# Modulation vector of a two-block layer: its column sums kept apart by partition groups and summed at two seams

## The chip, the cores and the metric

The kernel runs on one core of a Trainium2 chip. The metric is the device time of one execution in microseconds (us). A core has TensorE (PE, with its weight loads shown apart as PEld), VectorE (DVE), ScalarE (ACT), GpSimd (POOL) and SyncE (SP), whose queue issues nearly all transfers here.

## The reference, cut to what matters

The layer has two blocks. The second one is modulated by six vectors of D = 2048 columns, all from one product of the row `silu(c)` (1 x 2048) with `w_ada` (2048 x 12288):

```python
def second_block(x, c, w_in, w_out, ...):
    c_act = jax.nn.silu(c)
    for l in range(DEPTH):
        mod = (c_act @ w_ada[l] + b_ada[l])[:, None, :]
        sh1, sc1, g1, sh2, sc2, g2 = jnp.split(mod, 6, axis=-1)
        h = rms_norm(x, norm_mix[l]) * (1.0 + sc1) + sh1
        x = x + g1 * hybrid_mixer(h, ...)
        h = rms_norm(x, norm_ffn[l]) * (1.0 + sc2) + sh2
        x = x + g2 * conv_glu_ffn(h, ...)
```

The first block (a mixer, then a gated FFN) comes ahead of it and does not use `mod`. All is float32; the large products are made from high and low parts of their operands, three products for one.

## The kernel before, in words

The stages follow one another on one core: first mixer (to about 420 us), gated FFN `Glu` (to 908 us), its down projection `Down` (to 1148 us), second mixer (to 1612 us), convolution FFN (to 2101 us), its `Down` and the end. Each stage streams its weights through four raw buffers; ACT makes the high part of a half buffer (L289), DVE the low part (L297), three units ahead of the PE. Each engine's order is written out in the code by unit numbers; SP's order is written out too.

The product with `w_ada` runs beside them. Its 12288 columns are 12 groups ("leads") of 1024. For a group, class `Ada` loads 16 row blocks of 128 x 1024 in eight transfers of 1 MB (`load`, L498), and DVE multiplies each block by 128 values of `silu(c)`, one for a partition, and adds it to a 128 x 1024 accumulator (`product`, L516 and, for the first block, L518). The accumulator then has to be summed over its 128 partitions. Group 0 is gathered in the first mixer, groups 1 to 5 in `Glu`, 6 to 8 in `Down`, 9 in the second mixer, 10 and 11 in the convolution FFN. The sum is made in three ways:

- groups 0 to 5 (`turned`, `reduced`): right after the group, between two units of `Glu`, the PE transposes the accumulator in eight 128 x 128 pieces (L460) and DVE reduces them (L467) to eight columns of `modcols`;
- groups 6 and 7 (`Down.ada_sums`, L1953): at the seam from `Down` to the second mixer (here: seam 1), eight products with a column of ones each, and one addition of the bias by DVE at L1963. Group 8's accumulator is stored to memory there;
- groups 8 and 9 at the seam from the second mixer to the convolution FFN (seam 2): L3616 with ones, L460 by transposes; groups 10 and 11 by 128 x 512 products later (L3646).

Around seam 1 the order is: the PE's last products of `Down` (L1875), the sums, four early transposes (L2152), the rest of the sums, four transposes (L2141) that wait for rows scaled by ACT (L2117) and DVE (L2130), then the first products of the second mixer (L2216). DVE makes the mean there (L3172 to L3179), the factors 1 + scale (`modulation`, L3547) and a reciprocal (L3183) that waits for ACT's root (L2954). Seam 2 is built alike (L3745 to L3754, L2152, L2141, L608), with three idle transposes (L449, `keep_busy`) ahead of L2141. In the first mixer small vectors are loaded as rows (`packs`, tile `pack`), transposed by the PE one pack for a unit (L945) and copied by DVE to `col` (L1332).

## Time and profile before

| | |
|---|---|
| median of 3 runs | 2351.67 us (2350.42 to 2352.06) |
| profiled execution | 2352.51 us, span 2350.7 us |
| mean granted TensorE clock | 0.997 |
| PE busy | 2337.8 us, 99% |
| PEld busy | 2151.6 us, 92% |
| DVE busy | 1616.4 us, 69% |
| ACT busy | 1153.2 us, 49% |
| DMA | 543.62 MB, mean 231 GB/s |

The span runs from the first to the last instruction; 1.8 us of the execution's time lie outside it. The PE is busy nearly throughout. Records of matmuls overlap, so the time that one costs in a stream is read from the starts or from the chain of waits, not from its own duration.

### The profile page before, as it was taken

How to read it: one execution, taken by the hardware profiler on the slowest of the kernel's cores; microseconds unless marked ns; L12 is line 12 of the kernel's file. 1: busy time of each engine (PE TensorE's matmuls, PEld its weight loads, DVE VectorE, ACT ScalarE, POOL GpSimd, SP SyncE). 2: the span in 40 equal slices, each digit the busy share in tenths (PEclk: the TensorE clock that was granted, in tenths of full speed). 3: DMA queues.
4: the chain of work that ended last, by engine and by line, in shares of the span. 5: the costliest groups of instructions: out<-in, count | busy, mean ns of one | idle time of the engine just before them, and what ended most of it. 6: DMA issues, size and time to landing. Idle time of an engine off the chain costs nothing.

```text
span 2350.7 us, 43754 instructions
## 1 busy us (share of the span) xinstructions
PE 2337.8 (99%) x17937; PEld 2151.6 (92%) x17937; DVE 1616.4 (69%) x1931; ACT 1153.2 (49%) x1510; POOL 5.1 (0%) x7
## 2 busy tenths in 40 slices
PE   9999999999999999999999999999999999999998
PEld 8889778999999999888999899888999999998887
DVE  5668568777777766877778455667878666665556
ACT  5565454534344344444764444546544445454444
POOL 0000000000000000000000000000000000000000
PEclk9999999999999999999999999999999999999999
DMA  8556567888888877898577545555778656665563
GB/s 308 167 179 197 159 234 271 278 282 297 282 282 295 282 242 263 316 324 315 175 279 269 163 130 153 196 200 187 283 255 295 208 179 206 196 206 197 192 192 117
DMA packets 233049, 543.62 MB, mean 231 GB/s; under 512 B 15610, under 2 KB 22596, under 8 KB 232260
## 3 DMA queue, kind: packets, MB, share of 16 engines
q1 hardware_dynamic: 232756, 540.97, 68.3%
q8 instruction: 110, 1.80, 0.3%
q10 hardware_dynamic: 144, 0.52, 0.1%
q14 instruction: 39, 0.32, 0.0%
HBM read 535.11 MB, written 6.32 MB: 230 GB/s over the span
## 4 chain that ended last, share of the span: by engine, by line
PE 98%; DVE 0%; ACT 0%; issue 0%; DMA 0%; SPq 0%; DVEq 0%; ACTq 0%
PE ps L330 37%; PE ps L1858 18%; PE ps L608 18%; PE ps L2216 16%; PE ps L1875 2%; PE ps L2509 0%; PE ps L1041 0%; PE ps L1053 0%; PE ps L1071 0%; PE ps L1083 0%; PE ps L2141 0%; PE ps L460 0%; PE ps L2744 0%; PE ps L1134 0%; PE ps L2921 0%
## 5 line engine op out<-in xcount | busy, mean ns | idle before, releaser
L297 DVE TENSOR_TENSOR weights_lo<-raw_weights,weights_hi 128x1024 fp32r<-128x1024 f32 x786 | 957.6, 1224 | 659.8 <-ACT weights_hi L289 658.0
L289 ACT ACTIVATE weights_hi<-raw_weights 128x1024 fp32r<-128x1024 f32 x782 | 827.2, 1062 | 1086.8 <-PE ps L330 446.4
L516 DVE SCALAR_TENSOR_TENSOR ada_acc<-ada_w,col,ada_acc 128x1024 f32<-128x1024 f32 x180 | 230.2, 1279 | 0.1
L330 PE MATMUL ps<-conv_x_hi,weights_hi 128*128 128x256 f32 x1280 | 198.0, 277 | 0.0
L330 PE MATMUL ps<-glu_x_hi,weights_hi 128*128 128x256 f32 x1280 | 197.7, 276 | 0.0
L330 PE MATMUL ps<-glu_x_hi,weights_lo 128*128 128x256 f32 x1280 | 197.2, 276 | 0.0
L330 PE MATMUL ps<-glu_x_lo,weights_hi 128*128 128x256 f32 x1280 | 197.2, 276 | 0.0
L330 PE MATMUL ps<-conv_x_lo,weights_hi 128*128 128x256 f32 x1280 | 197.2, 276 | 0.0
L330 PE MATMUL ps<-conv_x_hi,weights_lo 128*128 128x256 f32 x1280 | 197.2, 276 | 0.0
L330 PEld LDWEIGHTS ps<-conv_x_hi,weights_hi 128*128 128x128 f32 x1280 | 169.1, 188 | 1.0 <-issue 1.0
L330 PEld LDWEIGHTS ps<-glu_x_hi,weights_hi 128*128 128x128 f32 x1280 | 169.0, 188 | 0.0
L330 PEld LDWEIGHTS ps<-glu_x_lo,weights_hi 128*128 128x128 f32 x1280 | 168.9, 188 | 0.0
L330 PEld LDWEIGHTS ps<-glu_x_hi,weights_lo 128*128 128x128 f32 x1280 | 168.9, 188 | 0.0
L330 PEld LDWEIGHTS ps<-conv_x_hi,weights_lo 128*128 128x128 f32 x1280 | 168.9, 188 | 0.0
L330 PEld LDWEIGHTS ps<-conv_x_lo,weights_hi 128*128 128x128 f32 x1280 | 168.9, 188 | 0.0
L2216 PE MATMUL ps<-m_x_hi,weights_hi 128*128 128x256 f32 (+1 forms) x576 | 94.9, 288 | 0.1
L3800 DVE SCALAR_TENSOR_TENSOR conv_y<-ps,conv_taps,conv_y 128x255 f32<-128x255 f32 (+1 forms) x176 | 72.7, 476 | 29.8 <-ACT conv_y L3732 28.8
L2216 PE MATMUL ps<-m_x_lo,weights_hi 128*128 128x256 f32 (+1 forms) x576 | 89.8, 279 | 0.0
L2216 PE MATMUL ps<-m_x_hi,weights_lo 128*128 128x256 f32 (+1 forms) x576 | 89.2, 277 | 0.5 <-issue 0.5
L1858 PE MATMUL ps<-weights_hi,down_hi 128*128 128x512 f32 x288 | 89.0, 390 | 0.5 <-DVE stat L3804 0.2
L1858 PE MATMUL ps<-weights_hi,down_lo 128*128 128x512 f32 x288 | 88.7, 389 | 0.0
L1858 PE MATMUL ps<-weights_lo,down_hi 128*128 128x512 f32 x288 | 88.7, 389 | 0.0
(560 smaller groups left out, 3635.3 us busy)
## 6 DMA issues: line engine op xcount, KB each, us to landing
raw_weights<-in_w_in_dram SPq DMA_DIRECT2D x202, 512.0 KB, 5.0
ada_w<-in_w_ada_dram SPq DMA_DIRECT2D x96, 1024.0 KB, 6.1
raw_weights<-in_w_ffn_up_dram SPq DMA_DIRECT2D x176, 512.0 KB, 4.6
raw_weights<-in_w_gate_dram SPq DMA_DIRECT2D x88, 512.0 KB, 4.6
raw_weights<-in_w_up_dram SPq DMA_DIRECT2D x88, 512.0 KB, 4.6
raw_weights<-in_w_down_dram SPq DMA_DIRECT2D x88, 512.0 KB, 5.7
raw_weights<-in_w_ffn_down_dram SPq DMA_DIRECT2D x88, 512.0 KB, 4.3
raw_weights<-in_w_out_dram SPq DMA_DIRECT2D x64, 512.0 KB, 5.1
```

The lines of the kernel that those rows point to most:

```text
L289: kit.nc.scalar.activation(kit.slots(n, i)[0], raw, ACT.Copy).then_inc(kit.w_hi, 1)
L297: kit.nc.vector.tensor_tensor(lo, raw, hi.bitcast(F32), ALU.subtract).then_inc(kit.w_lo, 1)
L330: ins = nc.tensor.matmul(out, lhsT=lhsT, rhs=rhs, start=start and m == 0, stop=(k == KT - 1 and m == 2), skip_group_check=True)
L516: step = nc.vector.scalar_tensor_tensor(acc, w, c, acc, ALU.mult, ALU.add)
L608: ins = nc.tensor.matmul(out, lhsT=lhsT, rhs=rhs, start=start and m == 0, stop=ends and m == 2, skip_group_check=True)
L1858: ins = nc.tensor.matmul(kit.ps[:, 4 * t + 2 * half + q, :], lhsT=lhsT, rhs=rhs, start=(k == 0 and m == 0), stop=ends and m == 2, skip_gro ...
L1875: ins = nc.tensor.matmul(kit.ps[:, 4 * t + 2 * half + q, :], lhsT=lhsT, rhs=w[:, q * UN:(q + 1) * UN], start=False, stop=k == w_tiles - 1 ...
L2216: ins = nc.tensor.matmul(out, lhsT=lhsT, rhs=rhs, start=start and m == 0, stop=ends and m == 2, skip_group_check=True)
L3800: nc.vector.scalar_tensor_tensor(y[:, j, q, b:S], self.tile(j, q)[:, 0:S - b], taps[:, j, tap, q:q + 1], y[:, j, q, b:S], ALU.mult, ALU.ad ...
```

## The change

Groups 0 to 7 now share one accumulator. Partition 16g + r belongs to group g: each transfer brings 16 rows of `w_ada` with the first 8192 columns, cut by group into 8 x 16 partitions, and the multiplier is a column in which 16 values of `silu(c)` are repeated eight times (`c_oct`, 128 such columns). After 128 steps one set of eight products with an indicator (`oct`, 128 x 8) gives all 64 columns. Groups 8 and 9 share another accumulator by halves (`c_half`, `half`, 128 x 2) in the same manner; its first half stays in the accumulator that is continued in the second mixer. Groups 10 and 11 are as before. The sums between the units of `Glu` and the additions of the bias behind them go. The 16 columns of a group are copied to a fixed tile in `Glu` (`c_turn`), since its loop counts groups. Each 1 MB transfer becomes two of 512 KB with a semaphore of their own. In the first mixer one more pack (`c_oct`, 128 x 128) is transposed one unit after the last; it waits until DVE has repeated its rows in the tile `pack` and copied the pack ahead of it.

```diff
     def load(self, sp, lead, j, m):
-        sp.dma_start(self.w[:, m % 2, :, :], w[2 * m * P:2 * (m + 1) * P, ds(2 * UN * lead + 2 * UN * j, 2 * UN)]
-                     .rearrange("(k p) n -> p k n", p=P)).then_inc(kit.ada_w[m % 2], 16)
+        for s in (2 * m, 2 * m + 1):
+            sp.dma_start(self.w[:, m % 2, s % 2, :], self.source(lead, j, s)).then_inc(kit.ada_w[s % 4], 16)
...
+    def source(self, lead, j, s):
+        w = self.kit.ins["w_ada_2"][0]
+        if lead < 8:
+            rows = w[ds(OCT * (16 * lead + s) + 16 * OCT * j, OCT), 0:16 * UN]
+        elif lead < 10:
+            rows = w[HALF * (16 * (lead - 8) + s):HALF * (16 * (lead - 8) + s + 1), 16 * UN:20 * UN]
...
+        return rows.rearrange("r (g n) -> g r n", n=2 * UN)
...
+    def sums(self, pe, bank, mask, acc):
+        kit, (a, b) = self.kit, self.kit.at[mask]
+        n = b - a
         for q in range(8):
+            step = kit.nc.tensor.matmul(kit.ps[:, bank, n * q:n * (q + 1)], lhsT=acc[:, q * P:(q + 1) * P],
+                                        rhs=kit.c(mask), start=True, stop=True)
...
-            mid = (lambda: self.ada.turned(pe, self.lead, j)) if summed else None
-                if summed and s == begun:
-                    self.ada.reduced(dve, self.lead, j)
                 if half is not None and s % 2 == begun:
-                    self.ada.product(dve, self.lead, j, 8 * half + s // 2)
+                    q = 8 * half + s // 2
+                    if q == 0:
+                        a = COLS["c_oct"] + 16 * self.lead
+                        dve.wait_ge(kit.ada_acc, 16 * self.lead + 16 * j)
+                        nc.vector.tensor_copy(self.c_turn[:, :], kit.col[:, ds(a + 16 * j, 16)]).then_inc(self.s_c, 1)
+                        dve.wait_ge(self.s_c, 1 + j)
+                    self.ada.product(dve, self.lead, j, q, c=self.c_turn[:, q:q + 1])
...
     def sync(self, sp):            # Down
-        sp.wait_ge(kit.ada_sum, self.lead)
-        sp.dma_start(self.final_w[:, :], self.final_src).then_inc(kit.loaded, 16)
+                if k == 12:
+                    sp.wait_ge(kit.ada_acc, 16 * self.lead + 1)
+                    self.load_final(sp)
...
     def pack_out(self, dve, n):
+        if n == len(self.packs) - 2:
+            dve.wait_ge(self.s_packs, 16 * sum(len(p[0]) for p in self.packs[1:]))
+            self.kit.nc.vector.tensor_copy(self.pack[:, 0, :].rearrange("p (g r) -> p g r", r=OCT),
+                                           self.c_rows[:, :].unsqueeze(1).broadcast_to([P, P // OCT, OCT])
+                                           ).then_inc(self.s_cwide, 1)
...
     def vector(self, dve):         # second mixer
+        self.down.ada_summed(dve)
         modulation(kit, 0)
...
     def scale_sums(self, pe):
-        for q in range(8):
-            step = kit.nc.tensor.matmul(kit.ps[:, 1, q:q + 1], lhsT=mixer.accs[:, 0, q * P:(q + 1) * P],
-                                        rhs=kit.c("ones")[:, 0:1], start=True, stop=True)
-        step.then_inc(kit.ada_sum, 1)
-        pe.wait_ge(mixer.s_xlast, ST)
-        turn_sums(kit, mixer.accs[:, 1, :], 2).then_inc(kit.ada_sum, 1)
+        pe.wait_ge(self.mixer.s_accs, 16)
+        pe.wait_ge(self.kit.pair_free[0], self.uses[0] + 1)
+        self.ada.sums(pe, 1, "half", self.mixer.acc_back)
```

The PE's order in `Glu`, between two units (names: `ps` the accumulation banks, `cst` the constants with the identity, `glu_x_hi/lo` the stage's operand). Before:

```order
L330 MATMUL ps<-glu_x_lo,weights_hi 128x256 x4
L330 MATMUL ps<-glu_x_hi,weights_lo 128x256 x4
L460 MATMUL ps<-cst,ada_acc 128x128 [waits ada_acc]
L460 MATMUL ps<-cst,ada_acc 128x128 x7
L330 MATMUL ps<-glu_x_hi,weights_hi 128x256 [waits weights_lo]
```

and at the same place now:

```order
L335 MATMUL ps<-glu_x_lo,weights_hi 128x256 x4
L335 MATMUL ps<-glu_x_hi,weights_lo 128x256 x4
L335 MATMUL ps<-glu_x_hi,weights_hi 128x256 [waits weights_lo]
L335 MATMUL ps<-glu_x_hi,weights_hi 128x256 x3
L335 MATMUL ps<-glu_x_lo,weights_hi 128x256 x4
```

The eight transposes have gone and nothing stands in their place. The PE's order at seam 1 (`m_scaled` are the rows to be transposed). Before:

```order
L1875 MATMUL ps<-down_last_hi,glu_x_lo 128x512
L1953 MATMUL ps<-cst,ada_acc_98 128x1 [waits ada_acc,square_sums,first_sems_cleared]
L1953 MATMUL ps<-cst,ada_acc_98 128x1 x7
L1953 MATMUL ps<-cst,ada_acc_99 128x1 x2
L2152 MATMUL ps<-cst,m_scaled_126 128x128 [waits rows_scaled0,square_sums]
L2152 MATMUL ps<-cst,m_scaled_126 128x128 [waits rows_scaled0] x3
L1953 MATMUL ps<-cst,ada_acc_99 128x1 x6
L2141 MATMUL ps<-cst,m_scaled_126 128x128 [waits rows_scaled1,rows_scaled0]
L2141 MATMUL ps<-cst,m_scaled_126 128x128
```

and now:

```order
L1873 MATMUL ps<-down_last_hi,glu_x_lo 128x512
L513 MATMUL ps<-cst,ada_acc_oct 128x8 [waits ada_acc,square_sums,first_sems_cleared]
L513 MATMUL ps<-cst,ada_acc_oct 128x8 x7
L2139 MATMUL ps<-cst,m_scaled_127 128x128 [waits rows_scaled0,square_sums]
L2139 MATMUL ps<-cst,m_scaled_127 128x128 [waits rows_scaled0] x3
L2128 MATMUL ps<-cst,m_scaled_127 128x128 [waits rows_scaled1,rows_scaled0]
L2128 MATMUL ps<-cst,m_scaled_127 128x128
```

Half of the sums have gone, among them all that stood between the early transposes and the waiting ones. DVE's order at the same seam, before and now (one piece each; `modT` holds the factors, `stat` the statistics):

```order
L3179 SCALAR_TENSOR_TENSOR stat<-stat 128x1 [waits square_sums,dve_order]
L3547 SCALAR_TENSOR_TENSOR modT<-modcols,col 128x16
L3183 RECIPROCAL stat<-stat 128x2 [waits m1_x_in0,dve_order]
L2130 TENSOR_SCALAR m_scaled_126<-x_weighted,stat 128x256 [waits token_scales] x2
L2130 TENSOR_SCALAR m_scaled_127<-x_weighted,stat 128x512 [waits token_scales]
```

```order
L3160 SCALAR_TENSOR_TENSOR stat<-stat 128x1 [waits square_sums,dve_order]
L523 TENSOR_TENSOR modcols<-ps,col 128x8x8 [waits ada_sum]
L3526 SCALAR_TENSOR_TENSOR modT<-modcols,col 128x16 [waits ada_out]
L3165 RECIPROCAL stat<-stat 128x2 [waits c_rows_repeated,dve_order]
L2117 TENSOR_SCALAR m_scaled_127<-x_weighted,stat 128x256 [waits token_scales] x2
```

The addition that brings the sums out of `ps` stands ahead of the factors, and the factors wait for it.

## Rows read from the trace of the kernel before

**Rows 1.** The page, part 1: busy time (share of the span) and instructions.
```profile
PE 2337.8 (99%) x17937; PEld 2151.6 (92%) x17937; DVE 1616.4 (69%) x1931; ACT 1153.2 (49%) x1510; POOL 5.1 (0%) x7
```
**Rows 2.** The page, part 4: the chain that ended last, shares by engine.
```profile
PE 98%; DVE 0%; ACT 0%; issue 0%; DMA 0%; SPq 0%; DVEq 0%; ACTq 0%
```
**Rows 3.** The chain in `Glu`, in order of time: start us, us, what.
```profile
514.28 0.87 PE ps L460 x8
515.16 87.12 PE ps L330 x768
602.27 0.87 PE ps L460 x8
...
867.12 40.87 PE ps L330 x360
```
**Rows 4.** The accumulator's instructions: ns min/median/max, first and last start us.
```profile
L516 DVE SCALAR_TENSOR_TENSOR ada_acc<-ada_w,col,ada_acc x180: 1273/1279/1287, 342.2 to 1827.2; 128x1024 f32<-128x1024 f32 x180
...
L460 PE MATMUL ps<-cst,ada_acc x48: 272/273/273, 427.8 to 866.8; 128*128 128x128 f32 x48
...
L518 DVE TENSOR_SCALAR ada_acc<-ada_w,col x12: 744/746/749, 337.7 to 1744.2; 128x1024 f32<-128x1024 f32 x12
```
**Rows 5.** `Glu` by windows: us, PE, PEld, DVE, ACT, POOL, PEclk, DMA share, GB/s.
```profile
510.00:900.00 390.00, 390.00 (x3441) 390.00 (x3441) 284.27 (x238) 158.66 (x152) 0.00 (x0) 1.00 0.80 276
```
**Rows 6.** The page, part 6: the transfers of `w_ada`.
```profile
ada_w<-in_w_ada_dram SPq DMA_DIRECT2D x96, 1024.0 KB, 6.1
```
**Rows 7.** The chain at seam 1.
```profile
1147.75 2.12 PE ps L1953 x20
1149.87 0.50 PE ps L2152 x4
1150.37 2.08 PE ps L1953 x12
1152.45 0.95 PE ps L2141 x4
```
**Rows 8.** DVE at seam 1, timeline.
```profile
1150.21 0.17 DVE L3547 SCALAR_TENSOR_TENSOR modT<-modcols,col 128x16 f32<-128x16 f32 x1
1150.63 0.17 DVE L3183 RECIPROCAL stat<-stat 128x2 f32<-128x2 f32 x1 [0.25 <-ACT stat L2954]
1150.83 1.01 DVE L2130 TENSOR_SCALAR m_scaled<-x_weighted,stat 128x256 f32<-128x256 f32 x3
```
**Rows 9.** Seam 1 by windows, columns as in Rows 5.
```profile
1147.30:1149.60 2.30, 2.30 (x21) 2.22 (x21) 2.03 (x6) 1.98 (x5) 0.00 (x0) 1.00 0.01 4
...
1150.60:1153.40 2.80, 2.80 (x13) 2.41 (x13) 1.18 (x4) 1.14 (x3) 0.00 (x0) 0.50 0.96 228
1153.40:1157.20 3.80, 3.74 (x18) 3.74 (x18) 3.70 (x8) 3.20 (x6) 0.00 (x0) 0.50 0.84 319
```
**Rows 10.** The chain at seam 2.
```profile
1612.57 1.68 PE ps L3616 x16
1614.25 0.93 PE ps L460 x8
1615.18 0.33 PE ps L449 x3
...
1615.63 0.32 PE ps L2141
```
**Rows 11.** Seam 2 by windows, columns as in Rows 5.
```profile
1612.30:1615.60 3.30, 3.21 (x30) 2.97 (x28) 2.50 (x11) 1.54 (x4) 0.00 (x0) 1.00 0.72 225
1615.60:1619.00 3.40, 2.88 (x20) 2.44 (x21) 2.87 (x8) 3.03 (x7) 0.00 (x0) 1.00 0.64 249
```
**Rows 12.** Seam 2, DVE, then the PE's next weight load, timeline.
```profile
1614.36 0.17 DVE L3627 TENSOR_TENSOR modcols<-ps,col 128x8 f32<-128x8 f32 x1 [0.50 <-PE ps L3616]
1614.44 0.15 DVE L3749 SCALAR_TENSOR_TENSOR stat<-stat 128x1 f32<-128x1 f32 x1
...
1615.60 0.47 PEld L2141 LDWEIGHTS ps<-cst,conv_scaled 128*128 128x128 f32 x4 [0.33 <-ACT conv_scaled L2117]
```
**Rows 13.** First mixer: the transposition of a pack in the chain.
```profile
57.95 0.08 PE ps L945
```
**Rows 14.** First mixer, DVE timeline: the copy of the last pack.
```profile
60.28 0.25 DVE L1332 COPY col<-ps 128x96 f32<-128x96 f32 x1
```
**Rows 15.** First mixer, PE timeline: the unit after next begins.
```profile
60.65 0.61 PE L608 MATMUL ps<-weights_hi,m_x_hi 128*128 128x512 f32 x2
```

More of the change, by code:

```diff
@@ L503, in product, with scalar @@
+    def scalar(self, lead, s):
+        name, first = ("c_oct", 0) if lead < 8 else ("c_half", 8) if lead < 10 else ("c_2", lead)
+        return self.kit.cols(name, 16 * (lead - first) + s)
+    def product(self, dve, lead, j, s, acc=None, prior=None, c=None):
         nc, kit = self.kit.nc, self.kit
         m, k = s // 2, s % 2
-        if s == 0 and self.stored:
-            dve.wait_ge(kit.ada_sum, lead - 1)
-            dve.wait_ge(self.stored, 16)
-        elif s == 0 and lead and acc is None:
-            dve.wait_ge(kit.ada_sum, lead + j)
@@ L827, in sync @@
         for n in range(1, len(self.packs)):
-            for at, to, width, src in self.packs[n][0]:
-                sp.dma_start(self.pack[at:to, n, 0:width], src).then_inc(self.s_packs, 16)
+            tile = self.c_rows if n == len(self.packs) - 1 else self.pack[:, n, :]
+            for at, to, lo, hi, src in self.packs[n][0]:
+                sp.dma_start(tile[at:to, lo:hi], src).then_inc(self.s_packs, 16)
         bias = self.mem["bias_dram"].ap()
@@ L944, in turn_pack @@
         _, w, _ = self.packs[n]
-        kit.nc.tensor.transpose(kit.ps[:, 6, 0:w], self.pack[0:w, n, :], kit.c("ident")[0:w, 0:w]
-                                ).then_inc(self.s_packT, 1)
+        last = n == len(self.packs) - 1
+        if last:
+            pe.wait_ge(self.s_cwide, 1)
+        rows = self.pack[0:w, 0 if last else n, :]
+        kit.nc.tensor.transpose(kit.ps[:, 6, 0:w], rows, kit.c("ident")[0:w, 0:w]).then_inc(self.s_packT, 1)
     def spread_scale(self, at):
@@ L3263, in vector_side @@
         if n in self.ADA:
-            self.ada.product(dve, self.lead, 0, self.ADA.index(n))
+            s = self.ADA.index(n)
+            self.ada.product(dve, self.lead, 0, s, prior=None if s else self.down.accs[1])
     def added_out(self, dve, p):
@@ L3825, in program @@
         junk = t("y_squares", 80, [P, ST, D])
-        accs = [t(f"ada_acc_{6 + n}", a, [P, 2 * UN])[:, :] for n, a in enumerate((56, 60, 106))]
+        accs = [t(f"ada_acc_{n}", a, [P, 2 * UN])[:, :] for n, a in (("oct", 56), ("half", 60))]
         def wide_head(w):
```

222 lines of the change are left out of this document (83 added, 139 removed).

## The prediction

> **What bounds the kernel now.** I read the page's shares first: the PE is busy for 99% of the span, DVE for 69% [rows 1]. A busy PE is not proof, so the chain of waits comes second: 98% of it is PE work [rows 2]. Only what shortens the PE's own list, or one of the few places where it waits, can move the time. The chain in `Glu` shows what a sum between two units costs: 87.12 us of stage products, then 0.87 us for eight transposes, then products again, with no idle time between them [rows 3]. The last places to read are the two seams, where the order of small steps decides [rows 7 to 12].
>
> **The change part by part.**
>
> *Transposes between units of `Glu`.* There are 48 in the accumulator's list, so six sets of eight, one for each of the groups 0 to 5 [rows 4]. Each set takes 0.87 us of the chain [rows 3]. All of it is on the path: 6 x 0.87 = 5.2 us. Nothing takes their place in the order. What is late next would be the weights' low parts from DVE, but DVE is busy for 284 of 390 us in this stage, and the PE waited for nothing in it (390.00 us busy) [rows 5]. So I count the whole 5.2 us as gained, with bounds of 4.8 (a little given back at the joints) and 5.3.
>
> *DVE's share.* Six reductions and one at seam 2 go. Eight first steps become additions: 1279 instead of 744 to 746 ns, + 0.53 us each [rows 4]. A copy of 16 columns and a wait for it come for each of five groups. In `Glu` this is about even for each group and lies under the PE's stream, with 106 us of DVE's time free there [rows 5]. In `Down` and the second mixer three first steps, 1.6 us, are spread over 700 us. Cost 0; if the cover were gone, at most the 1.6 us and the copies.
>
> *Transfers.* 80 of the 96 transfers of 1 MB [rows 6] read other addresses, all 96 become two. A piece for one partition remains 4 KB, and the bytes are the same. The DMA engines are busy for 0.80 of `Glu` [rows 5]. Cost 0, with the bound as a rival below.
>
> *Seam 1, the PE.* Before, 20 records of thin products, four early transposes, 12 more records, then the transposes that wait for scaled rows [rows 7]. Each product shows as two records. Twenty records took 2.12 us of the chain, 106 ns each; 12 records took 2.08 us, 173 ns each, because the granted clock fell from 1.00 to 0.50 (2.4 to 1.2 GHz) at about 1150.6, after three microseconds in which the PE had made hardly anything but one-column products [rows 7, 9]. Now 16 records remain, all ahead of the early transposes. With 8 columns instead of one I take the same 106 ns, since the weight load is the same; if the columns counted, seven more for each record would still be a small part of the 128 of a transpose, at 109 ns (0.87/8) [rows 3]. So the sums end 0.4 us earlier, and the early transposes are followed directly by the waiting ones. DVE begins to scale the second rows at 1150.83 in three steps of together 1.01 us [rows 8], the first third done at about 1151.17. The waiting transposes began in the chain at 1152.45 because the thin products still stood ahead of them [rows 7]. They can now start at about 1151.3, plus what DVE adds.
>
> *Seam 1, DVE.* The addition of 64 columns and its wait now stand ahead of the factors and the reciprocal. DVE was idle for 0.25 us there, until ACT's root came [rows 8]. The addition is like the 0.17 us steps around it, plus some 0.1 us for 64 strided elements and about 0.1 us for the wait: 0.3 to 0.4 us, of which the idle time hides 0.25. I take + 0.1, at most + 0.4. Queued behind it are the reciprocal and the scaled rows, for which the PE waits.
>
> *Seam 1, sum.* In hand: between the first piece of scaled rows (1151.2) and the end of the thin products (1152.45) lie 1.25 us, less 0.2 for the handover, less 0.1 for DVE: about 0.95 at most. From there the PE runs at half the clock until about 1157.3 [rows 9]. If that end stays where it is, an earlier start is worth half of itself, 0.45; if it moves along, 0.95. Without any fall of the clock before, there would be about 0.1 in it. I take - 0.5, bounds 0 and - 1.0.
>
> *Seam 2.* The eight transposes (0.93 us) went before three idle ones and 0.33 us of waiting for scaled rows [rows 10, 12]. Without them the PE waits longer at the same place: gain 0. The 16 thin records remain. DVE's addition (1614.36) now has to finish before the next step of the mean (1614.44, 0.08 us later) [rows 12]: that step starts after the addition's 0.17 us and hands on, so the chain mean, root, reciprocal, scaled rows, PE is late by 0.1 us. Cost + 0.1, bounds 0 and + 0.2. The reduction and the second set of factors that stood later on DVE there go, under PE work.
>
> *First mixer.* One more pack is transposed: 0.1 us, as the 0.08 of the one before [rows 13]. It stands one unit later, and the next unit started at 60.65 [rows 15]. DVE starts the copy of the pack before at 60.28 (0.25 us) [rows 14]. Ahead of it now stands the copy that repeats the rows, of the same kind and size, so both are done at about 60.85, and the PE waits 0.25 us. Together + 0.35, bounds + 0.1 and + 0.6. Three more small transfers on SP's queue and one activation of 160 columns lie in units whose weights are made three units (8 us) ahead: 0.
>
> *Entry of `Down`.* A wait for the additions and the addition go. The chain has no more than 0.1 us in it: 0.
>
> Sum: - 5.2 - 0.5 + 0.1 + 0.35 = - 5.25 us; I take - 5.1, since handovers rather cost than give. Against the profiled execution (2352.5 us) that is 2347.4; it was 0.8 us above the median of the runs, so against this (2351.7) it is 2346.6.
>
> **The clock at seam 2, the rival that the sum hides.** In seam 2 the clock stayed at 1.00 through 3.3 us of thin products, transposes and a short wait, and through the next 3.4 us [rows 11]. In seam 1 it fell after thin products that were broken only by four transposes (0.50 us) [rows 7, 9]. The change takes out of seam 2 just the eight transposes that stood between thin products and waiting, and leaves 1.7 us of thin products, 0.33 us of idle transposes and about 1.3 us of waiting. So it may fall there now. The price from seam 1: 3.8 us of dense work at half the clock before it rose [rows 9], half of it lost, 1.9 us. The time would be 2346.6 + 1.9 = 2348.5.
>
> The Trainium skill ("TensorE: Matmul & The Clock Gate", Part 4: PE-mode transpose) says that transposes do not count as busy for the clock as products do. By that, seam 2 was as quiet before as it is now, and the change would not make a fall there likelier. This trace has one row for each side: four transposes did not keep the clock at seam 1, eight more stood in seam 2 where it stayed. The rule alone would leave the sum as it is and lower the chance of this rival.
>
> **Other rivals.**
> - *More at seam 1* (chance 0.08): with the thin products halved, the clock does not fall there. The 3.8 us of dense work at half the clock [rows 9] would give back 1.9 us, and the first transposes (0.95 for four, against 0.5 for four early ones [rows 7]) another 0.4: about 2344.3. For it: less thin work. Against: what replaces it is waiting.
> - *The stream was held by something else* (0.05): if the sets of transposes covered time that DVE needed, the PE would wait at the same joints and most of the 5.2 us would come back: about 2351. Against: no wait of the PE in `Glu`, DVE 73% busy [rows 5].
> - *Slower* (0.03): the transfers in eight column pieces of 16 rows run slower. From one set of transposes to the next (88 us) some 24 MB come at 276 GB/s [rows 3, 5], and 8 of them are a group of `w_ada`: a third, 0.27 of the 0.80 share. Once they take over 1.75 times as long, the share passes 1 and the PE waits; at twice as long it is 1.07, and the 470 us of `Glu` grow by 7%, 33 us: 2380. Against: the pieces stay at 4 KB and their rows lie closer together.
>
> **How the numbers follow.** Forecast as summed: 0.6; the clock falls at seam 2: 0.24; the others 0.08, 0.05, 0.03. The likeliest case gives 2346.6. The bounds of its terms add to - 6.2 at one end (- 5.3 - 1.0 + 0 + 0.1) and - 4.0 at the other (- 4.8 + 0 + 0.2 + 0.6), and the runs shown differ by 1.6 us among themselves. With the clock rivals on either side the range is 2344.7 to 2349.4. A change of 0.2%, 4.7 us, is about what a measurement of this kernel can tell from none, and the forecast lies just beyond it, below 2347.0. Of the forecast's 0.6 I put 0.45 beyond it, with the 0.08 and a few hundredths of the rest: faster 0.57, within 0.2% 0.40, slower 0.03.
>
> **What would show it.** Right: in `Glu` the chain shows products without a break and the PE busy to the full; `Down` begins 5.2 us earlier, less what the first mixer added, so at about 903.3; seam 1, from the last dense product to the first of the second mixer, is shorter by about 0.9 us; the PE's wait ahead of the first waiting transposes at seam 2 grows from 0.33 to about 1.3 us. Wrong: a clock of 0.50 in seam 2 beside a gain under 4 us; a wait of the PE for DVE's low parts in `Glu`; transfers of `w_ada` whose two halves take clearly more than the 6.1 us of the whole [rows 6]; a wait of over 0.5 us for the repeated rows in the first mixer.

## The result, and the profile after

The changed kernel took 2873.7 us in the median (2857.1 to 2891.9), the kernel before 2351.8 in the same comparison: a ratio of 1.222, 95% interval 1.214 to 1.231. Forecast were 2346.6 us. It is not slightly slower, it is 522 us slower, and the forecast had given "slower" a chance of 0.03. The profiled execution took 2857.1 us, its span is 2855.3.

The page of the changed kernel, part 1 (answers to [rows 1]), the shares of part 4 by engine ([rows 2]), and two lines of part 6 ([rows 6] and a kind of stage weights):
```profile
PE 2481.5 (87%) x17866; PEld 2259.3 (79%) x17866; DVE 1603.4 (56%) x1927; ACT 1149.0 (40%) x1511; POOL 5.1 (0%) x7
...
PE 52%; DMA 35%; DVE 6%; SPq 4%; issue 2%; ACT 1%; DVEq 0%; ACTq 0%
...
ada_w<-in_w_ada_dram SPq DMA_DIRECT2D x192, 512.0 KB
...
raw_weights<-in_w_gate_dram SPq DMA_DIRECT2D x88, 512.0 KB, 18.0
```
The chain was 98% PE work; now transfers make 35% of it. The stage weights, which the change does not touch, need 18.0 us from issue to landing for the gate, 18.9 and 18.4 for `w_up` and `w_down`; in the kernel before the page had 4.6, 4.6 and 5.7 for them. For `ada_w` the page gives no landing time.

The chain of the changed kernel inside `Glu` (answers to [rows 3]), and what waited for `ada_w` in the whole kernel (us in total, times):
```profile
611.02 20.58 DMA ada_w<-in_w_ada_dram
...
635.18 1.28 DVE ada_acc L505
636.46 2.28 DVE weights_lo L302 x2
...
639.53 21.32 DMA ada_w<-in_w_ada_dram
```
```profile
  DVE ada_acc L505: 382.0, 56
  DVE ada_acc_half L505: 145.8, 15
```
The chain stays on one transfer for 20 to 21 us. DVE stands at its accumulating instruction, in program order the low parts of the weights are behind it, and the PE is behind those. The accumulating instruction itself is what it was: 1283 ns against 1279 [rows 4].

Windows of the changed kernel, columns as in [rows 5]: `Glu`, and the time of groups 8 and 9. Then the head of the DMA view of the second window in 40 slices (tenths of the mean share of 16 engines; GB/s):
```profile
510.00:900.00 390.00, 312.89 (x2445) 308.64 (x2446) 203.99 (x177) 112.26 (x107) 0.00 (x0) 0.89 0.79 207
1310.00:1490.00 180.00, 91.70 (x266) 68.83 (x265) 45.53 (x46) 24.82 (x32) 0.00 (x0) 0.71 0.32 106
```
```profile
DMA  3111541111951113511118711117211158111159
GB/s 100 53 53 52 164 129 54 53 53 71 283 183 53 52 56 134 162 53 53 52 52 249 237 53 52 52 53 218 83 53 53 53 181 284 76 53 56 53 180 270
```
This is the telling pair of rows. In `Glu` the share is as before (0.79 against 0.80 [rows 5]) while the bytes fall from 276 to 207 GB/s. Later the DMA engines look idle, a tenth busy, and the rate stands still at 52 or 53 GB/s for many slices. Two of sixteen engines are 0.125 of the share, and 53 GB/s over two are 26.5 GB/s each; e1 below reaches 406 GB/s in one slice of 5 us, 25.4 for each of sixteen. So in those slices two engines work at their full rate and fourteen stand. The source of groups 8 and 9 has the group as its outermost dimension, of size 2; that of groups 0 to 7 has it at 8.

The two rows of windows say different things. Fewer engines at their full rate lower the share and the rate together: 106 GB/s at 0.32 are 331 GB/s for a full share, near the 345 (276 / 0.80) of `Glu` before. In the changed `Glu` it is 207 / 0.79, 262. There the engines were also slower for each byte; how much is worked out under e3 and e4.

The queue that issues the transfers was held up as well. The transfers of `ada_w` in the second window (issue time in ns, least, median, most), and a piece of SP's timeline there:
```profile
L487 SPq DMA_DIRECT2D ada_w<-in_w_ada_dram x13: 787/9849/12712, 1308.7 to 1461.7; - x13
...
1344.12 14.44 SPq L258 DMA_DIRECT2D raw_weights<-in_w_down_dram  x4
1358.60 11.94 SPq L487 DMA_DIRECT2D ada_w<-in_w_ada_dram  x2
```
To issue one took 9.8 us in the median, which is what 512 KB need at 53 GB/s (9.9 us); in e1 below it is 346 ns. Stage weights are issued by the same queue, so they came late in two ways: issued late and, once issued, landed late.

The Trainium skill says it outright ("DMA: Bandwidth & Descriptors", "Why a DMA increments its semaphore by 16 and not by 1", How many engines): the number of engines is the largest up to 16 that divides the slowest dimension of both access patterns, and they are the lowest-numbered ones. By that, 8 and 2 engines; for 2 the 53 GB/s at a tenth of the share agree, for 8 no row shows the number of engines by itself. The prediction had not weighed this rule.

### The profile page after: what moved, and what is told of

Read it like the earlier page. It is cut to its first block, busy times and chain, and to the rows that moved or that the text cites. A ratio compares the mean times of both kernels' runs of the same rounds, so it can differ in the third digit from the quotient of the medians.

```text
span 2855.3 us, 43835 instructions
## 1 busy us (share of the span) xinstructions
PE 2481.5 (87%) x17866; PEld 2259.3 (79%) x17866; DVE 1603.4 (56%) x1927; ACT 1149.0 (40%) x1511; POOL 5.1 (0%) x7
## 4 chain that ended last, share of the span: by engine, by line
PE 52%; DMA 35%; DVE 6%; SPq 4%; issue 2%; ACT 1%; DVEq 0%; ACTq 0%
DMA ada_w<-in_w_ada_dram 28%; PE ps L335 17%; PE ps L579 11%; PE ps L2203 10%; PE ps L1856 8%; DVE weights_lo L302 3%; DMA raw_weights<-in_w_in_dram 3%; SPq L258 3%; DMA raw_weights<-in_w_out_dram 2%; PE ps L1873 1%; DVE ada_acc L505 1%; SPq L487 1%; DMA raw_weights<-in_w_gate_dram 1%; DMA raw_weights<-in_w_down_dram 1%; DVE ada_acc_oct L505 0%
## 5 line engine op out<-in xcount | busy, mean ns | idle before, releaser
L335 PE MATMUL ps<-glu_x_hi,weights_hi 128*128 128x256 f32 x1280 | 221.8, 299 | 111.9 <-DVE weights_lo L302 111.9
L335 PEld LDWEIGHTS ps<-glu_x_hi,weights_hi 128*128 128x128 f32 x1280 | 189.2, 208 | 118.3 <-DVE weights_lo L302 115.1
L505 DVE SCALAR_TENSOR_TENSOR ada_acc<-ada_w,glu_c,ada_acc 128x1024 f32<-128x1024 f32 x80 | 102.6, 1282 | 287.8 <-DMA ada_w<-in_w_ada_dram 285.4
L335 PE MATMUL ps<-glu_x_lo,weights_hi 128*128 128x256 f32 x1280 | 214.1, 293 | 0.0
L335 PE MATMUL ps<-glu_x_hi,weights_lo 128*128 128x256 f32 x1280 | 212.2, 291 | 0.0
L335 PE MATMUL ps<-conv_x_hi,weights_hi 128*128 128x256 f32 x1280 | 198.0, 277 | 0.0
L335 PE MATMUL ps<-conv_x_lo,weights_hi 128*128 128x256 f32 x1280 | 197.2, 276 | 0.0
L335 PE MATMUL ps<-conv_x_hi,weights_lo 128*128 128x256 f32 x1280 | 197.2, 276 | 0.0
L335 PEld LDWEIGHTS ps<-glu_x_lo,weights_hi 128*128 128x128 f32 x1280 | 186.5, 205 | 0.0
L335 PEld LDWEIGHTS ps<-glu_x_hi,weights_lo 128*128 128x128 f32 x1280 | 184.4, 203 | 0.0
L335 PEld LDWEIGHTS ps<-conv_x_hi,weights_hi 128*128 128x128 f32 x1280 | 169.1, 188 | 1.0 <-issue 1.0
L335 PEld LDWEIGHTS ps<-conv_x_lo,weights_hi 128*128 128x128 f32 x1280 | 168.9, 188 | 0.0
L335 PEld LDWEIGHTS ps<-conv_x_hi,weights_lo 128*128 128x128 f32 x1280 | 168.9, 188 | 0.0
L505 DVE SCALAR_TENSOR_TENSOR ada_acc<-ada_w,col,ada_acc 128x1024 f32<-128x1024 f32 x60 | 76.8, 1280 | 109.1 <-DMA ada_w<-in_w_ada_dram 95.4
L1856 PE MATMUL ps<-weights_hi,glu_x_hi 128*128 128x512 f32 x192 | 71.9, 461 | 75.5 <-DVE weights_lo L302 75.5
L2203 PEld LDWEIGHTS ps<-m_x_hi,weights_hi 128*128 128x128 f32 (+1 forms) x576 | 88.0, 211 | 53.3 <-DVE weights_lo L302 50.9
L1856 PEld LDWEIGHTS ps<-weights_hi,down_hi 128*128 128x128 f32 x288 | 57.2, 204 | 71.3 <-issue 58.8
L1856 PEld LDWEIGHTS ps<-weights_hi,glu_x_hi 128*128 128x128 f32 x192 | 41.7, 225 | 89.3 <-issue 81.0
## 6 DMA issues: line engine op xcount, KB each, us to landing
raw_weights<-in_w_up_dram SPq DMA_DIRECT2D x88, 512.0 KB, 18.9
raw_weights<-in_w_down_dram SPq DMA_DIRECT2D x88, 512.0 KB, 18.4
```

What stands on the lines that cost most here:

```text
L335: ins = nc.tensor.matmul(out, lhsT=lhsT, rhs=rhs, start=start and m == 0, stop=(k == KT - 1 and m == 2), skip_group_check=True)
L505: step = nc.vector.scalar_tensor_tensor(acc, w, c, acc if prior is None else prior, ALU.mult, ALU.add)
L1856: ins = nc.tensor.matmul(kit.ps[:, 4 * t + 2 * half + q, :], lhsT=lhsT, rhs=rhs, start=(k == 0 and m == 0), stop=ends and m == 2, skip_gro ...
L2203: ins = nc.tensor.matmul(out, lhsT=lhsT, rhs=rhs, start=start and m == 0, stop=ends and m == 2, skip_group_check=True)
```

## The experiments

All were compared with the kernel before on the same chip (2351.6 to 2354.8 us in the median). Theory after the result: the outermost dimension sets the number of engines. Rivals: the rows' addresses, the doubled number of transfers, or something on PE or DVE.

**e1_plain_rows.** Everything of the change stays except the source of the transfers: groups 0 to 9 read plain blocks of 128 rows, so the sums are not those of the reference.
```
-        if lead < 8:
-            rows = w[ds(OCT * (16 * lead + s) + 16 * OCT * j, OCT), 0:16 * UN]
-        elif lead < 10:
-            rows = w[HALF * (16 * (lead - 8) + s):HALF * (16 * (lead - 8) + s + 1), 16 * UN:20 * UN]
+        if lead < 10:
+            rows = w[P * s:P * (s + 1), ds(2 * UN * lead + 2 * UN * j, 2 * UN)]
```


> The changed kernel with one thing different: every transfer of w_ada for groups 0 to 9 reads 128 whole rows of one group's 1024 columns, as groups 10 and 11 do (same 512 KB, same tile, same count and order of transfers; the accumulated values are therefore not those of the reference). Theory A (a transfer whose address pattern has 8 or 2 as its slowest dimension runs on 8 or 2 of the 16 DMA engines, and all of the lost time comes from that): 2346 to 2348 us, the forecast of the prediction, PE clock 0.997, no wait of DVE for ada_w. Theory B (twice the number of transfers, each half as large, with issues and semaphores of their own, is what costs): still far above 2352, near 2870. Theory C (the seams or the shared accumulator cost part of it): 2355 to 2450.

2347.4 us, ratio 0.9981 (0.9971 to 0.9991). All 526 us hang on how `w_ada` is read; twice as many transfers cost nothing that shows beside the forecast (2346.6), and the rest of the change is worth some 4.2 us. The transfers of `ada_w` land after 5.4 us by the page, and `Glu` is undisturbed:
```profile
510.00:900.00 390.00, 390.00 (x3444) 390.00 (x3443) 283.22 (x240) 161.47 (x153) 0.00 (x0) 1.00 0.81 278
```

**e2_rows_slowest.** The whole reference, with the row as outermost dimension: 16 rows x 8 pieces, so partition 8r+g instead of 16g+r; groups 8 and 9 as two transfers of 64 rows to 64 partitions each.
```
-        return rows.rearrange("r (g n) -> g r n", n=2 * UN)
+        return rows.rearrange("r (g n) -> r g n" if lead < 8 else "r (g n) -> g r n", n=2 * UN)
...
+                for g in range(2):
+                    sp.dma_start(self.w[HALF * g:HALF * (g + 1), m % 2, s % 2, :], src[g]).then_inc(kit.ada_w[s % 4], 16)
```


> The changed kernel with the same bytes of w_ada read from the same addresses into the same number of partitions, but with the rows as the slowest dimension. Groups 0 to 7: partition 8r + g instead of 16g + r (indicator and repeated multipliers follow), so the transfer's slowest dimension is 16 instead of 8. Groups 8 and 9: layout as it was, each 512 KB transfer made as two of 64 rows, so 64 instead of 2. It computes all of the reference. Theory A (number of engines by the slowest dimension): 2346 to 2350 us; half transfers issue 32 more times on SP, hidden. Theory D (the addresses: 16 or 64 rows of 48 KB pitch with 4 KB pieces side by side are slow to read): stays near 2870, at most a little better.

2440.3 us (2409.9 to 2454.7), ratio 1.033 (1.027 to 1.040). Neither theory had this: A had said 2346 to 2350, D near 2870. Sixteen as outermost dimension gives back 433 of the 526 us, but 93 remain. Its `Glu`, from a run with a span of 2452.9 us, the longest of its four:
```profile
510.00:900.00 390.00, 365.10 (x3100) 361.29 (x3101) 259.02 (x226) 145.90 (x140) 0.00 (x0) 0.98 0.98 263
```
The share is 0.98 for 263 GB/s, where e1 moved 278 with 0.81: a full set of engines, each slower. That is a second effect. The profile of e5 below, from the fastest of its runs, which has the same eight-group transfers and plain ones for groups 8 and 9, shows it too:
```profile
510.00:900.00 390.00, 368.84 (x3169) 365.14 (x3168) 260.39 (x227) 146.81 (x141) 0.00 (x0) 0.99 1.00 264
```

**e3_oct_only** and **e4_half_only.** The changed kernel with groups 8 and 9 plain, and with groups 0 to 7 plain.
```
e3:  -            rows = w[HALF * (16 * (lead - 8) + s):HALF * (16 * (lead - 8) + s + 1), 16 * UN:20 * UN]
     +            rows = w[P * s:P * (s + 1), ds(2 * UN * lead + 2 * UN * j, 2 * UN)]
e4:  -            rows = w[ds(OCT * (16 * lead + s) + 16 * OCT * j, OCT), 0:16 * UN]
     +            rows = w[P * s:P * (s + 1), ds(2 * UN * lead + 2 * UN * j, 2 * UN)]
```

> The changed kernel with groups 8 and 9 read as whole rows (values not those of the reference); groups 0 to 7 keep eight column pieces of 16 rows. It prices the 128 transfers with slowest dimension 8. Theory A: 8 of 16 engines carry 1 MB of w_ada and 1 MB of stage weights for each group of about 88 us, against 1.5 MB before, and bursts of a transfer take twice as long; the traced stage from 424 to about 1095 us in the changed kernel suggests about 2352 + 165 (FFN) + 25 (mixer) + 60 (down, two of three groups) = 2600 us. The stretch of groups 8 in the down projection becomes normal.

> The changed kernel with groups 0 to 7 read as whole rows (values not those of the reference); groups 8 and 9 keep two column pieces of 64 rows. It prices the 32 transfers with slowest dimension 2. Theory A: 512 KB over 2 engines at about 26.5 GB/s each is 9.9 us for a transfer, and the stage's own weights queue behind on these two engines; 32 transfers cost about 32 x 9.9 = 320 us less what is hidden, so about 2600 us; the sum of the two excesses (this one and that of the run with groups 0 to 7 alone) equals the whole 520 us within 10%. In that stretch the transfer rate stands at 53 GB/s.

2608.5 us (ratio 1.110) and 2606.0 (1.108). Above e1 these are 261 and 259 us, together 520 of the 526: two separate losses of one kind, the smaller volume on the fewer engines costing as much. In `Glu`, e4 is undisturbed (1.00, 0.81 and 278 as in e1) and e3 is not; a stretch of e4, 1200 to 1400 us, shows the 52 GB/s again in the DMA view:
```profile
510.00:900.00 390.00, 297.89 (x2297) 293.21 (x2297) 189.38 (x165) 107.02 (x103) 0.00 (x0) 0.89 0.79 194
```
```profile
GB/s 62 261 172 52 56 52 162 255 254 53 48 13 354 386 95 82 208 218 202 121 199 3 344 314 386 61 139 144 52 52 52 156 215 52 52 53 223 143 138 51
```
What the transfers cost the engines can be read from part 3 of the pages (packets, MB, share of 16 engines), e1, e3 and e4:
```profile
q1 hardware_dynamic: 234260, 539.96, 68.6%
...
q1 hardware_dynamic: 233236, 539.95, 68.3%
...
q1 hardware_dynamic: 233812, 539.96, 62.3%
```
The bytes are the same. Times the spans (2345.9, 2642.5 and 2602.7 us) these are 1609, 1805 and 1622 us of all sixteen engines. The 67 MB of groups 0 to 7 cost about 196 us at e1's rate in `Glu` (278 GB/s at 0.81), and e3 adds 196 to them: transfers with 8 outermost took about twice the engine time for each byte, beside being on half of the engines. The 17 MB of groups 8 and 9 cost 49 us and e4 adds 12: with 2 outermost the time for a byte grew by about a quarter. These are estimates from rounded shares.

**m1_sixteen_rows, m2_halves_and_turned, m3_engines.** To find the second effect, each kernel issues four kinds of transfer in turn, each from its own line, for groups 0 to 5, and plain ones for 6 to 9. The sums are not the reference's, and each of these kernels ran once; a kind has 24 transfers. The sources of m1's kinds 1 to 3, and m2's kind 1:
```
w[ds(16 * (16 * L + s) + 256 * j, 16), 0:16 * UN]   "r (g n) -> r g n"                    # 16 rows, adjacent
w.rearrange("(r q) c -> r q c", q=128)[:, 16 * L + s + 16 * j, 0:16 * UN]  "-> r g n"      # 16 rows, 128 apart
w[ds(...), :]  "r (g n) -> r g n" with n=3 * UN, [:, :, 0:2 * UN]                          # pieces 6 KB apart
w[128 * s:128 * (s + 1), ...]  "(m i) c -> i m c" with i=16                                # turned block
```


> Four ways of reading w_ada side by side in one kernel, in the pairs of transfers issued at the same instant (each 2 x 512 KB, 16 engines), for the groups before Down; every kind has its own line, and each kind comes twice in a group of 16. The values are not the reference's. Kinds: 0 plain blocks of 128 rows; 1 sixteen adjacent rows, eight adjacent pieces of 4 KB from each (as in e2_rows_slowest); 2 sixteen rows that lie 128 rows apart, eight adjacent pieces; 3 sixteen adjacent rows, eight pieces that lie 6 KB apart. In e1_plain_rows a transfer landed 5.4 us after its issue, in e2_rows_slowest 15.4. Theory N (what slows the engines is that all 16 read from rows that lie close together): kinds 1 and 3 land late, 9 us or more, kinds 0 and 2 at 5 to 6.5. Theory C (what slows them is that one engine reads 32 KB in a row of adjacent addresses): kinds 1 and 2 land late, kinds 0 and 3 early. Time of the kernel: between those of the two, 2350 to 2400 us.

> As m1_sixteen_rows, with other kinds: 0 plain blocks of 128 rows, of which an engine reads eight adjacent rows; 1 the same blocks turned, so that engine i reads rows i, 16+i, 32+i and so on, and the 16 engines stand on 16 adjacent rows at any time; 2 sixty-four adjacent rows, two pieces each; 3 sixty-four rows that lie 32 rows apart, two pieces each. Theory N: it is the place of the 16 engines at one time that counts, so kind 1 lands late like the sixteen rows (9 us or more) although it reads the plain blocks; kind 2 somewhat late (7 to 12), kind 3 at 5 to 6.5. Theory B (bytes of a transfer drawn from a small stretch of w_ada, whoever reads them): kind 1 like kind 0 at 5 to 6.5, kind 2 late. Time 2348 to 2390 us.

> As m1_sixteen_rows, with other kinds: 0 plain (slowest dimension 128); 1 as in the changed kernel, slowest dimension 8, sixteen adjacent rows; 2 slowest dimension 8, sixteen rows 128 rows apart; 3 slowest dimension 4, thirty-two adjacent rows and four pieces. Theory E (the slowest dimension sets the number of engines, each at its full rate of some 26 GB/s): a pair of 1 MB takes 1 MB / (8 x 26 GB/s) = 5 us on eight engines and 10 us on four, beside the stage weights that wait on the same engines; so kinds 1 and 2 land later than kind 0 by a factor of two, kind 3 by a factor of four. If nearness adds to it, kind 1 lands later than kind 2 by half again; if not, the same. Time 2450 to 2700 us.

Landing times by line (least, median, most us) of m1: kinds 0, 1, 2, 3:
```profile
DMA to landing us min/median/max: 3.8/5.7/9.6
...
DMA to landing us min/median/max: 5.0/6.9/16.1
...
DMA to landing us min/median/max: 5.6/7.5/13.2
...
DMA to landing us min/median/max: 4.4/5.4/10.1
```
The same of m2: plain, turned, 64 rows near, 64 rows spread:
```profile
DMA to landing us min/median/max: 4.0/5.8/9.9
...
DMA to landing us min/median/max: 5.0/7.3/16.5
...
DMA to landing us min/median/max: 4.5/5.8/9.8
...
DMA to landing us min/median/max: 4.0/5.7/7.8
```
Both theories of addresses fall. Rows 128 apart are as slow as adjacent ones (7.5, 6.9), which N forbids; adjacent rows with pieces 6 KB apart are as fast as plain (5.4). C fits m1, but the turned block of m2 has no adjacent pieces and is slow (7.3). B said that it would be like plain, and falls too. What the three slow kinds share is a source that begins with a dimension of exactly 16; the fast "6 KB apart" has one even stride over all 128 pieces, so its dimensions can fold into 128. That they do is read from its issue time on SP, 345 ns in the median as for plain (348), where the slow kinds take 556 to 569. The landing times were lower than I had written (9 us), I take it because only a part of the transfers is slow here. The kernels took 2346.5 and 2347.3 us, less than the 2350 and 2348 that I had put as their least. The windows of `Glu` of m1 and of m2 show what they occupy:
```profile
510.00:900.00 390.00, 390.00 (x3444) 390.00 (x3443) 283.32 (x239) 160.66 (x152) 0.00 (x0) 1.00 0.88 278
```
```profile
510.00:900.00 390.00, 390.00 (x3444) 390.00 (x3443) 283.50 (x239) 160.65 (x152) 0.00 (x0) 1.00 0.85 277
```
`w_ada` is 0.27 of the share, one kind of four 0.07. Two slow kinds add 0.07 and one adds 0.04: each takes 1.5 to 1.6 times as long. All of it at 1.6 would make 0.81 + 0.16 = 0.97. e2 shows 0.98 and e5 1.00, but at 263 and 264 GB/s instead of 278; for each byte that is a `w_ada` at 1.8 to 1.9 times. So where all of it is slow, it is slower still.

m3 took 2550.9 us. Its transfers on 8 and 4 engines have no landing row, but DVE's waits for each kind have:
```profile
  DVE ada_acc L514: 13.5, 6
...
  DVE ada_acc L514: 65.5, 18
...
  DVE ada_acc L514: 92.4, 12
...
  DVE ada_acc L514: 125.0, 22
```
Plain, outermost 8 with rows near, 8 with rows 128 apart, 4: the order is that of the number of engines. Between the two eights nothing is decided: the one with rows 128 apart is issued right before and right after the transfers on 4 engines, whose issue alone takes 3.7 us in the median, and its waits may hold part of theirs. Factors of two and four, as I had written them, cannot be read from it.

**m4_sixteen_chunks, e5_oct_sixteen_engines, e6_half_one_transfer, e7_split_plain.** The theory now is P: the writing side. By it the 16 engines write to 16 separate places when the first dimension is 128; with exactly 16, or with only 64 partitions, pairs of engines would write through one port. m4's kind 2 keeps the plain addresses but does not fold; e7 keeps the plain addresses and cuts a transfer of groups 8 and 9 at partition 64; e6 puts 64 rows x 2 pieces in one transfer.
```
m4, kind 1:  w[32 rows, 0:8 * UN]    "r (g n) -> r g n"                       # 32 x 4
m4, kind 2:  w[144 rows, ...]        "(i k) n -> i k n" with k=9, [:, 0:8, :] # 16 x 8
e6:          w[64 rows, 16 * UN:20 * UN]  "r (g n) -> r g n"                  # 64 x 2
e7:          w[P * s:P * (s + 1), ...]    "(g r) n -> g r n" with g=2, one transfer for each g
```


> As m1_sixteen_rows, again four kinds of transfer side by side on lines of their own, all on 16 engines. m1 and m2 showed: sixteen rows of eight adjacent pieces are slow whether the rows are adjacent or 128 apart (7.5 and 6.9 us in the median against 5.7), plain blocks turned so that the slowest dimension is 16 are slow too (7.3), while 16 adjacent rows of pieces 6 KB apart (which fold into one even dimension of 128) and 64 rows of two pieces are not (5.4, 5.8). Kinds here: 0 plain (dimension 128); 1 thirty-two adjacent rows, four adjacent pieces (dimensions 32 x 4); 2 sixteen chunks of eight adjacent rows of which every ninth is left out (16 x 8: the addresses nearly those of the plain block, but the dimensions do not fold); 3 as kind 3 of m1 with every second row (16 x 8, does not fold either). Theory P (a source whose slowest dimension is exactly 16 gives each engine eight neighbouring partitions in the kernel's memory to write, and the engines get in each other's way at writing; where the rows lie makes no difference): kinds 2 and 3 land late at about 7 us or more, kind 1 as kind 0. Theory A (the addresses read decide): kind 2 like kind 0, kind 3 like kind 3 of m1, both at 5.3 to 6. Time 2345 to 2352 us.

> e2_rows_slowest with groups 8 and 9 read as whole blocks of 128 rows, one transfer each (their values are then not the reference's): only the eight-group transfers keep the slowest dimension 16. The 93 us that e2_rows_slowest stands above e1_plain_rows split into the share of the eight groups and that of the two halves. Both theories: most of it belongs to the eight groups, since PE stood idle from 500 to 1150 us there. 2405 to 2435 us.

> e1_plain_rows with groups 8 and 9 read as 64 rows of two pieces, the row as slowest dimension (64), in one transfer of 128 partitions; groups 0 to 7 plain (values not the reference's). From kind 2 of m2 (5.8 us as the plain blocks): 2346 to 2349 us by theory P as well as by theory A. If it is over 2352, 64 x 2 has a cost that m2 did not show.

> e1_plain_rows with each transfer of groups 8 and 9 cut in two, of 64 partitions each, as in e2_rows_slowest, but of the whole blocks' rows: what is read is what e1 reads, and only the 64 partitions that each transfer writes are as in e2 (11.3 us from issue to landing there, 5.4 in e1). Values not the reference's. Theory P (the writing side): landing of these transfers 8 us or more although their addresses are plain; the kernel some microseconds over e1: 2350 to 2375. Theory A (addresses read): landing 4 to 6, kernel 2346 to 2349.

m4 (2347.3 us), kinds 0 to 3, then e7's transfers to 64 partitions:
```profile
DMA to landing us min/median/max: 4.6/5.6/9.9
...
DMA to landing us min/median/max: 3.9/5.4/12.8
...
DMA to landing us min/median/max: 5.5/7.5/11.0
...
DMA to landing us min/median/max: 5.5/7.2/11.4
```
```profile
DMA to landing us min/median/max: 3.9/10.1/19.1
```
Both 16 x 8 kinds are slow (7.5, 7.2), one of them at nearly plain addresses, the other being m1's fast kind 3 with its fold broken; 32 x 4 is not (5.4). The kinds stand in the same places of a group as in m1, where kind 1 was slow and kind 3 fast, so the place is not the cause. (The expectation of m4 gives m1's two values in the wrong order: adjacent rows took 6.9, rows 128 apart 7.5.) Theory A falls: the addresses that are read do not decide. Plain addresses written to 64 partitions at a time take 10.1 us, where e1's transfers of the same groups took 5.5. This is weaker than it looks, since e7 also has twice as many transfers of half the size there, and no run has those without the 64 partitions.

e7 as a whole: 2354.7 us (2345.9 to 2364.4), ratio 1.0013 (0.9999 to 1.0027), 7 us over e1. e6: 2347.1 us, ratio 0.9981, as e1: 64 rows x 2 costs nothing. e5: 2424.3 us (2411 to 2443), ratio 1.034 (1.029 to 1.039). So the eight groups alone cost 77 us over e1. How much of e2's 93 belongs to the halves cannot be read from the times, whose ratios are the same (1.033 and 1.034). The traces do show a part: DVE waits for the halves' transfers 33.1 us in e2 and 1.9 in e5.

That it is the ports rests on shapes and not on a row that names a port. The Trainium skill ("SBUF — State Buffer", "Door 1: The DMA port swizzle") puts partitions four by four on sixteen ports and p and p+32 on the same one; the Trainium skill ("DMA: Bandwidth & Descriptors", "The descriptor swizzle") gives each engine in a 128-partition transfer a port of its own. If engine i has the neighbouring partitions 8i to 8i+7 instead, engines i and i+4 begin on one port; with 64 partitions only eight ports are in use. Both would give up to a factor of two. The shares show 1.5 to 1.9, the landing times 1.2 to 1.3 for the four kinds and 1.8 for e7. The same reasoning covers the changed kernel. With partition 16g + r, and engine g taking group g, engines 0 and 2 write to partitions 0 to 15 and 32 to 47, which are the same ports, while the two engines of the halves (0 to 63, 64 to 127) share none. The 2.0 and 1.2 worked out above fit that. Which engine writes where, and why 32 x 4 and 64 x 2 escape, no row shows.

**e8_half_rows.** A version from this: 32 half rows x 4 pieces, so that groups 0 to 3 and 6 to 9 share the first accumulator and no outermost dimension is 16; groups 4 and 5 as 64 rows x 2. They are the gate of the second mixer, so their sums move there.
```
+            halves = w.rearrange("r (h c) -> (r h) c", h=2)
+            rows = halves[ds(2 * OCT * (16 * lead + s) + 32 * OCT * j, 2 * OCT), 0:8 * UN]
         elif lead < 10:
+            rows = w[HALF * (16 * (lead - 8) + s):HALF * (16 * (lead - 8) + s + 1), 8 * UN:12 * UN]
...
+        if n == self.GATE1 - 1:
+            self.ada.sums(pe, 7, "half", self.acc_back)
```


> The whole reference again, with both shared accumulators, and every transfer in dimensions that go to 16 engines without a slowest dimension of 16: the eight-group transfer reads thirty-two half rows (row r, half h) of four pieces each, so partition 8r+4h+g holds groups 0 to 3 for h = 0 and 6 to 9 for h = 1 (32 x 4, as kind 1 of m4); groups 4 and 5 share the second accumulator as 64 rows of two pieces (64 x 2, as e6_half_one_transfer). Because groups 4 and 5 are the gate that the second mixer uses at about 1490 us, their 8 products of sums stand there instead of at the second seam, and the stored accumulator comes back at about 1470 us. Theory P: the transfers cost what the plain blocks cost, so the kernel is at e1_plain_rows, 2347.4, give or take 1.5 us for the moved sums (8 products of 0.25 us and a wait of about 0.5 us at 1487, against 1.6 us and a wait less at the second seam): 2345 to 2349, ratio 0.997 to 0.999. If reading half rows in another order of addresses mattered (theory A), the Glu stage would show a DMA share over 0.90 and waits on ada_w, and the kernel would stand over 2352.

2348.9 us (2347.8 to 2351.4), against 2352.1 of the kernel before in the same comparison: ratio 0.9985 (0.9976 to 0.9994). The whole reference, faster than both kernels by the interval, by 0.15%. `Glu` in it:
```profile
510.00:900.00 390.00, 390.00 (x3443) 390.00 (x3442) 283.24 (x240) 161.34 (x153) 0.00 (x0) 1.00 0.83 278
```

## Why the prediction was wrong

**The step that failed** is the one on transfers: "80 of the 96 transfers of 1 MB read other addresses, all 96 become two. A piece for one partition remains 4 KB, and the bytes are the same." It looked at the size of a piece and at the bytes, and not at the order of the dimensions. Cost taken: 0. Measured: 526 us, of which e3 and e4 show 261 for the groups with 8 outermost and 259 for those with 2.

The rival "Slower" had the right place, but kept the sixteen engines in mind, priced the case at 2380 and argued against it with the nearness of the rows, which m1 shows to make no difference. For groups 8 and 9 the price could have been had once two engines were in the sum: 32 transfers of 9.9 us are 317, less what is hidden, as e4's expectation has it; 259 were measured. For groups 0 to 7 the number of engines would not have been enough. Of the 0.80 share 0.27 are `w_ada`; on eight engines this is 0.54 beside 0.53 of the rest on the same engines, 1.07 as in the rival, and the same 33 us. With twice the time for each byte it is 1.08 beside 0.53, 1.61, and from its first products at L335 on `glu_x` to the start of `Down` e3 took 638 us against 435 in e1, 1.47 times as long. So the prediction lacked two things, fewer engines and a longer time for each byte, and did not look at SP's queue, which the slow transfers hold.

Two of its own signs of being wrong came true: the PE waits 111.9 us for the low parts of the weights at L335, and transfers took far over 6.1 us. The range, 2344.7 to 2349.4, was that of the terms it had, and had no room for the one it lacked.

**The other terms** can be read in e1, which has all of them and plain transfers. Forecast for them: 2346.6; measured 2347.4. The chain of e1 at the four places:
```profile
41.66 2.81 PE ps L577 x24
...
68.00 1.06 PE ps L1023 x8
```
```profile
904.15 217.89 PE ps L1854 x960
```
```profile
1139.95 3.87 PE ps L1871 x17
...
1147.48 0.93 PE ps L2126 x4
...
1148.48 4.25 PE ps L2201 x24
...
1153.16 2.75 PE ps L2201 x24
```
```profile
1606.31 1.70 PE ps L511 x16
...
1609.52 0.31 PE ps L2126
...
1611.38 4.16 PE ps L577 x20
...
1615.97 2.74 PE ps L577 x24
```
- *First mixer*, + 0.35 forecast. Between the same two places 26.34 us (41.66 to 68.00) against 26.01 before (40.24 to 66.25): + 0.33. Right. Both stand later than before by over a microsecond, and part of it is there with the very first weights (landed at 6.76 us against 6.32); I have no cause for it.
- *Transposes*, - 5.2. From there to the start of `Down`: 836.15 us against 841.87, - 5.7. Right in kind; 0.5 more than six sets, which I cannot place. `Down` begins at 904.15, forecast 903.3; the late start (1.4 us) less this 0.5 accounts for it.
- *Seam 1*, - 0.5, bounds to - 1.0. From the last dense product of `Down` to the second run of dense products: 9.34 us against 10.97, - 1.6. The term was too small, and its bound too: the waiting transposes began 3.66 us after the last dense product, against 4.70 before, so the whole of the time "in hand" came, and the clock, though it fell, was down for a shorter time (windows below, against 0.50 for 6.6 us in [rows 9]).
- *Seam 2*, + 0.1. From the sums to the second run of dense products: 9.66 us against 8.00, + 1.7. Here the rival of the clock came true. The PE waits 1.5 us, as foreseen (1608.00 to 1609.52), then 20 records take 4.16 us; before, 2.63. Its price had been 1.9.
- The second mixer between them is 0.7 us shorter, for which I have no cause.

```profile
1147.40:1150.60 3.20, 3.05 (x14) 2.62 (x15) 2.68 (x7) 2.78 (x7) 0.00 (x0) 0.54 0.91 311
1150.60:1152.70 2.10, 2.10 (x18) 2.10 (x18) 2.10 (x4) 1.01 (x2) 0.00 (x0) 0.88 0.19 72
...
1611.30:1615.50 4.20, 4.12 (x22) 4.12 (x23) 4.14 (x9) 2.35 (x5) 0.00 (x0) 0.59 0.08 18
```
So for the PE's list the sum was within a microsecond, partly by luck: two misses at the seams have opposite signs, and the late start takes away what the transposes and the second mixer gave beyond the forecast. The rule of the Trainium skill on transposes and the clock ("TensorE: Matmul & The Clock Gate", Part 4: PE-mode transpose), weighed in the prediction, gets a row that may speak against it: with eight transposes less at seam 2 the clock fell (0.59) where it had stayed at 1.00 [rows 11], so here they had helped to hold it, or the longer wait in their place let it go; no run parts the two.

What is shown of the loss is that most of it hangs on the outermost dimension of the source and not on the addresses: e2 reads the same addresses in another order of dimensions and gets back 433 of the 526 us, and e3 and e4 split the loss into 8 and 2. How its size splits between fewer engines, time for each byte and the held queue was not measured apart, and the ports are argued, not shown.

## What to carry to other kernels

When a change touches the access pattern of a transfer, read its outermost dimension before its bytes. With 128, or 32 x 4 and 64 x 2 pieces, it was free; with exactly 16, or 64 partitions for each transfer, the bytes took 1.5 to 1.9 times as long; with 8 and 2 it cost 11% of this kernel each. In a profile there are three different signs. A rate that stands still at one value beside a low share (53 GB/s at 0.1) is few engines. A rate that is low for its share (207 at 0.79 beside 276 at 0.80) is engines that are slow for each byte. A third is the issuing queue: microseconds for an issue that took 0.35 before. A change whose gain is 0.2% of the PE's list deserves its largest unexamined "cost 0" to be worked out first, since there a mistake has no bound.

## What the runs showed of the hardware

- Transfers whose source began with 2 went at 52 to 53 GB/s in all (changed kernel, e4); e1, with 128 in the first dimension, reached 406 in a slice of 5 us.
- To issue a transfer on 2 engines held SP's queue for 9.8 us in the median, one on 4 engines 3.7 us (m3).
- Sixteen rows x 8 pieces, near or 128 rows apart, took 6.9 to 7.5 us from issue to landing where plain blocks took 5.6 to 5.8; 32 x 4 and 64 x 2 took 5.4 and 5.7 to 5.8.
- A transfer to 64 partitions (256 KB) landed after 10.1 us, one of 512 KB of the same rows to 128 after 5.5.
- Issuing a transfer on 16 engines with unfolded dimensions takes SP's queue 541 to 598 ns in the median, a plain one 346 to 348; in e8 this did not matter.
